# Two norm sums, eight spills and the row maxima of a two-block transformer kernel moved or recast

## The chip, the cores and the metric

The kernel runs on one core of a Trainium2 chip. The metric is the device time of one execution in microseconds (us). Five engines work side by side and meet at semaphores: TensorE (PE, matrix multiplies into PSUM), VectorE (DVE), ScalarE (ACT), GpSimd (POOL) and SyncE (SP, which here issues the weight loads). Each runs its own list of instructions in order.

## What is computed

The reference applies two blocks one after the other to a sequence of 1024 tokens of width 1024, all in float32. The first block mixes banded attention, a convolution and a recurrence, adds a feed-forward part and ends with a norm:

```
def hybrid_layer(x, ...):
    h = rmsnorm(x, norm1_g)
    z = jnp.einsum("bsd,dc->bsc", h, w_in)
    ...
    x = x + jnp.einsum("bsc,cd->bsd", mix, w_out)
    h2 = rmsnorm(x, norm2_g)
    ff = jnp.square(jax.nn.relu(jnp.einsum("bsd,df->bsf", h2, w_up)))
    return x + jnp.einsum("bsf,fd->bsd", ff, w_down)
```

The result goes through `rmsnorm(x, final_g)`. The second block puts 16 learned tokens in front (1040 in all) and runs two layers:

```
for l in range(DEPTH_2):
    h = rmsnorm_2(h_res, norm_gain[l])
    proj = h @ w_in[l]
    u_pool, z_pool, c_q, c_kv, k_rope, z_mla, g_pool, g_mla = jnp.split(proj, ...)
    y_pool = (pool_mix(u_pool, ...) * jax.nn.silu(z_pool)) @ pool_w_up[l]
    o_mla = mla(c_q, c_kv, k_rope, pos, ...)
    ...
    h_res = h_res + merged @ w_out[l]
```

`pool_mix` subtracts each value from running means over 2, 4, 8 and 16 steps, in four groups. `mla` is causal softmax attention with 8 heads; its softmax takes the maximum of each row of scores off before the exponential.

## The kernel before

Activations lie transposed: 128 channels on the partitions, time along the columns, in eight tiles. `X` is the residual, `Ah` and `Al` the rounded high and the low part of the normed activations, `R` 19 work rows (rows 8 to 15 are also `G`, the split inputs of small products), `S_` single columns. A float32 product is made of three rounded (fp32r) matmuls, high by high, high by low and low by high (`chunk_products`, L444; `piece_products`, L549). Weights come as a stream of units of 512 KB through two slots: SP loads one, POOL splits it into high (L388, L400) and low (L379) when the unit before it in the slot is used up. A unit is 128 output channels; its products accumulate in one of two slots of PSUM, `acc[:, 0]` and `acc[:, 1]`, which ACT or DVE must empty before the slot is taken again (`take`).

**Norms at the seams.** Where a residual is finished and normed at once, work goes in column pieces: two for attention's output (`CUTS1`, 512 columns each) and three around the second block (`CUTS_MID`, `CUTS2`, 348 each). `close_two` or `close_down` finish the residual piece by piece; `norm_pieces` on DVE and ACT adds the squares, and with the scale makes `Ah` and `Al` chunk by chunk (eight chunks of a piece); `open_two` on PE multiplies the chunks as they come by the next two units. The sum over channels is one f32 matmul with ones for each piece, `sum_piece` (L546). `open_two` first takes chunks 0 to 3 of piece 0 for unit 0, then the last piece's `sum_piece(n - 1)`, then for k = 0 to 7 unit 0's chunk k + 4 and unit 1's chunk k, and then the further pieces. The order of DVE and ACT is written out by hand:

```
NORM_ORDER = {
    2: (("add", 0), ("norm", 0, 0, 4), ("add", 1), ("norm", 0, 4, 6), ("norm", 0, 6, 8), ("norm", 1, 0, 8)),
...
NORM_SCALE_AFTER = {2: (0, 3), 3: (0, 3, 6)}
```

After the step with such a number ACT waits for the sum of the next piece and makes its scale (L1178, L1182). Within a "norm" step DVE multiplies (L1742), ACT copies to the high part (L1115) and DVE subtracts for the low part (L1735).

**The first layer's two norms.** The second block's first norm is taken of the first block's output before that output's own norm is applied, so two totals of squares are kept: the weighed one for the layer's norm, and the plain one (`R` row 16) for `final_g`. The plain total gets its last two squares after `norm_pieces` (L1430 on ACT, L2067 on DVE), PE sums it in two halves of 512 (L818, four instructions) after the wide unit j = 2, ACT makes the scale in `residual_scale` (L1443, L1446) after its eviction 1, DVE scales the eight residual tiles in `SPILL_ORDER` (L2071), and ACT spills them to DRAM (L1458) after its eviction 3. The pooling (`pool_mix`, L2086 to L2096 in DVE's list) writes over residual tiles, so it waits for all spills. It is followed by L2101, which empties the PSUM slot of the unit j = 4 and the next; PE wants that slot for j = 6. In the second layer the residual is spilled in one piece after the norm (L1436).

**The heads.** The 8 heads of a layer are interleaved: while head h is weighed, head g = h + 1 is projected and normed. PE, DVE and ACT each walk through 15 block steps n of a head with their own hand-written lists. Rough scores (one rounded product, L935 and L939) give the row maxima by `maximum` on DVE (L2219); `turn_maxima` on PE (L956) turns them from columns into a row, in three turns of a head: pc 0 at n = 10 of the head before, pc 1 at n = 0, pc 2 at n = 5. A turn has three f32 matmuls, each with one column of `S_` as weights and 128 columns of the identity moving (20 for the last tile of pc 2). ACT copies the row from partition 32 into row 32 of the queries. `rough_scores` for tile i also waits for `q_hi`, the cast L2198 in `query_norm`. `query_table` starts with L2185.

Of the kernel before, what the change touches and what calls it, by code (L numbers as in the profile page):

```python
# [10 lines left out]
ALU = mybir.AluOpType  # L11
# [137 lines left out]
def build(nc, xT, metaT, pos, params, consts, bands, lru_w, wstream, outT):  # L149
    with ExitStack() as ctx:  # L150
# [59 lines left out]
        extra0 = idr0 + 3 * P  # L210
# [216 lines left out]
        def _(pe):  # L427
# [176 lines left out]
            def open_two(ws, pieces, cuts):  # L604

                n, w = pieces
                lo0 = c["piece_lo"].n
                free0 = c["piece_free"].n
                c["piece_lo"].step(n * KC)
                c["piece_free"].step(2 * (n - 1))  # L610
                ahead = 4

                def begin(p, s):
                    if p < n - 1:
                        pe.wait_ge(sems["piece_free"], free0 + 2 * p + s + 1)
                    else:
                        take(s)

                def arrived(p, k):
                    pe.wait_ge(sems["piece_lo"], lo0 + KC * p + k + 1)  # L620

                next_unit()
                begin(0, 0)
                for k in range(ahead):
                    arrived(0, k)
                    piece_products(0, ws[0], 0, w, k, k == 0, False, (0, 1))
                await_low()
                for k in range(ahead):
                    piece_products(0, ws[0], 0, w, k, False, False, (2,))
                sum_piece(n - 1, cuts)  # L630
                next_unit()
                begin(0, 1)
                for k in range(KC):
                    if k + ahead < KC:
                        arrived(0, k + ahead)
                        piece_products(0, ws[0], 0, w, k + ahead, False, k + ahead == KC - 1)
                    piece_products(1, ws[1], 0, w, k, k == 0, False, (0, 1))
                await_low()
                for k in range(KC):
                    piece_products(1, ws[1], 0, w, k, False, k == KC - 1, (2,))  # L640
                for p in range(1, n):
                    for k in range(KC):
                        for s in range(2):
                            if k == 0:
                                begin(p, s)
                            if s == 0:
                                arrived(p, k)
                            ins = piece_products(s, ws[s], p, w, k, k == 0, k == KC - 1)
                            if p == n - 1 and k == KC - 1:
                                ins.then_inc(sems["unit_done"], 1)  # L650
# [152 lines left out]
            for l in range(LAYERS):  # L803
# [6 lines left out]
                open_two((ws(), ws()), PIECES2, CUTS_MID if l == 0 else CUTS2)  # L810
                for j in range(2, 8):
                    wide(j % 2, ws(), PIECES2)
                    if l == 0 and j == 2:
                        pe.wait_ge(sems["x1_total"], 1)
                        pe.wait_ge(sems["piece_scale"], c["piece_total"].value())
                        for p in range(2):
                            take_aux(p)
                            ins = nc.tensor.matmul(aux[:, p, :], ones, R[:, 16, CUTS1[p]:CUTS1[p + 1]],  # L818
                                                   start=True, stop=True)
                        ins.then_inc(sems["x1_summed"], 1)  # L820
# [123 lines left out]
                def turn_maxima(h, pc):  # L944
# [8 lines left out]
                    for i in range(3 * pc, 3 * pc + 3):  # L953
                        n = min(P, TP - P * i)
                        o = P * (i - 3 * pc)
                        ins = nc.tensor.matmul(acc_r[bank][32:33, o:o + n], S_[:, 16 + i:17 + i], ident[:, P - n:P],  # L956
# [130 lines left out]
        def _(act):  # L1087
# [337 lines left out]
            for l in range(LAYERS):  # L1425
                last = l == LAYERS - 1
                if l == 0:
                    norm_pieces(CUTS_MID, gain_root)
                    for s in range(2):
                        do(nc.scalar.activation(R[:, 13 + s, mid], X[:, KC - 2 + s, mid], ACT.Square), "x1_squared")  # L1430
# [24 lines left out]
                if l == 0:  # L1455
                    for i, j in enumerate(SPILL_ORDER):
                        act.wait_ge(sems["x1_done"], i + 1)
                        act.dma_start(spill_x[:, TP * j:TP * j + TP], X[:, j, :]).then_inc(sems["spilled"], 16)  # L1458
# [209 lines left out]
        def _(dve):  # L1668
# [386 lines left out]
            for slots in totals:  # L2055
                dve.wait_ge(sems[slots[3]], KC - 2)
                do(vec.tensor_tensor(slots[0], slots[0], slots[1 + (KC - 3) % 2], ALU.add), slots[3] + "_free")

            wide = slice(0, TP)
            for l in range(LAYERS):  # L2060
                last = l == LAYERS - 1
                if l == 0:
                    norm_pieces(CUTS_MID, lambda j: S_[:, 8 + j:9 + j], down=True)
                    do(vec.memset(R[:, 0:4, 0:16], 0.0), "to_act")
                    for s in range(2):
                        dve.wait_ge(sems["x1_squared"], s + 1)
                        do(vec.tensor_tensor(R[:, 16, mid], R[:, 16, mid], R[:, 13 + s, mid], ALU.add),  # L2067
# [146 lines left out]
                def maximum(h, i, p):  # L2214
# [4 lines left out]
                    do(vec.tensor_reduce(S_[:, col:col + 1], acc_r[rough_bank(i, p)][:, 0:n], AX, ALU.max, negate=True), "rough_max")  # L2219

                def maxima_of(pc):

                    if pc == 1:
                        do(vec.tensor_tensor(S_[:, 20:22], S_[:, 20:22], S_[:, 25:27], ALU.min), "max_ready")
                    else:
                        do(vec.tensor_tensor(S_[:, 24:25], S_[:, 24:25], S_[:, 30:31], ALU.min))
                        do(vec.tensor_tensor(S_[:, 22:25], S_[:, 22:25], S_[:, 27:30], ALU.min), "max_ready")
# [16 lines left out]
                do(vec.tensor_copy(ident_r, ident))  # L2244
                do(vec.tensor_copy(causal_r, C_[:, 384:512]))
# [232 lines left out]
```

## Time and profile before

| what | value |
|---|---|
| three timed runs | 3276.66, 3276.34, 3274.18 us; median 3276.34 |
| the profiled execution | 3276.7 us; span of its instructions 3274.9 us, mean granted clock of PE 0.975 |
| busy share of the span | PE 93%, PE weight loads 82%, DVE 43%, POOL 33%, ACT 23% |
| chain that ended last | PE 84%, DVE 11%, ACT 3%, issue 1% |

The span is the time from the first to the last instruction of the profiled execution; its own time beside it is measured in the same way as the three runs. PE is busy nearly throughout, so what counts is PE's own work, and the places where PE stands and waits for another engine.

### The profile page before, as it was taken

To read this page: it belongs to the slowest core of one execution; us is meant where nothing else is said; L and a number is where in the kernel's file an instruction comes from. 1 tells how busy PE (TensorE), PEld (TensorE's weight loads), DVE (VectorE), ACT (ScalarE), POOL (GpSimd) and SP (SyncE) were. 2 spreads that over 40 slices of the span, in tenths; PEclk is the share of its full clock that TensorE was granted. 3 is DMA by queue.
4 is the path that set the end of the run, shared out by engine and by line. 5 is a ranking of instruction groups with operands and counts; after the bars stand their busy time and mean duration, and the time that the engine had idled before them with its cause. 6 is when DMAs were issued, how large, how long until landed. Compare 5 with 4: busy or idle time off the path is not lost.

```text
span 3274.9 us, 41451 instructions
## 1 busy us (share of the span) xinstructions
PE 3041.6 (93%) x16392; PEld 2685.3 (82%) x16392; DVE 1424.4 (43%) x1818; ACT 738.0 (23%) x1332; POOL 1066.9 (33%) x1335
## 2 busy tenths in 40 slices
PE   6986679999999998699999899999999999899999
PEld 4764557777777787699999788889999999788899
DVE  4658456332222227520111666673720021766661
ACT  2143322000000003100110455511200111555510
POOL 2523013544444443333332211133433333211132
PEclk9998789999999999899999999999999999999999
DMA  2101011111111111211212000051211212100052
GB/s 107 45 33 36 1 71 46 52 45 49 47 45 45 45 52 33 98 39 46 99 51 79 33 14 14 14 190 39 105 52 46 98 46 81 37 14 14 14 183 78
DMA packets 47447, 182.62 MB, mean 56 GB/s; under 512 B 6081, under 2 KB 6209, under 8 KB 46913
## 3 DMA queue, kind: packets, MB, share of 16 engines
q1 hardware_dynamic: 31248, 113.19, 10.5%
q10 hardware_dynamic: 16048, 67.28, 5.4%
q8 instruction: 113, 1.85, 0.2%
q14 instruction: 38, 0.30, 0.0%
HBM read 150.06 MB, written 30.39 MB: 55 GB/s over the span
## 4 chain that ended last, share of the span: by engine, by line
PE 84%; DVE 11%; ACT 3%; issue 1%; DMA 0%; ACTq 0%; POOL 0%; DVEq 0%; SPq 0%; POOLq 0%
PE acc L451 60%; PE aux L1002 4%; PE acc L886 4%; PE acc L981 3%; PE acc L554 3%; PE acc L935 2%; PE acc L870 1%; PE acc L956 1%; DVE residual L1812 1%; PE acc L898 1%; DVE act_lo L1703 1%; PE acc L908 1%; PE acc L753 1%; DVE act_hi L1702 1%; DVE work L1742 1%
## 5 line engine op out<-in xcount | busy, mean ns | idle before, releaser
L379 POOL TENSOR_TENSOR w_lo<-w_raw,w_hi 128x256 fp32r<-128x256 f32 (+1 forms) x924 | 807.2, 905 | 17.2
L451 PE MATMUL acc<-act_hi,w_hi 128*128 128x348 f32 (+1 forms) x2896 | 712.5, 346 | 61.4 <-DVE work L2101 24.0
L451 PE MATMUL acc<-act_lo,w_hi 128*128 128x348 f32 (+1 forms) x2896 | 708.6, 345 | 0.0
L451 PEld LDWEIGHTS acc<-act_hi,w_hi 128*128 128x128 f32 x2896 | 507.1, 189 | 111.0 <-issue 55.0
L451 PE MATMUL acc<-act_hi,w_lo 128*128 128x348 f32 (+1 forms) x2896 | 562.3, 344 | 0.0
L399 POOL TENSOR_TENSOR small<-shape_consts 128x1 f32<-128x1 f32 x192 | 45.8, 239 | 1530.2 <-PE acc L451 1420.4
L451 PEld LDWEIGHTS acc<-act_lo,w_hi 128*128 128x128 f32 x2896 | 508.7, 189 | 39.8
L451 PEld LDWEIGHTS acc<-act_hi,w_lo 128*128 128x128 f32 x2896 | 490.3, 188 | 39.5
L451 PE MATMUL acc<-ff_split,w_hi 128*128 128x512 f32 (+1 forms) x1376 | 309.9, 374 | 10.8 <-DVE ff_split L1703 10.8
L451 PEld LDWEIGHTS acc<-ff_split,w_hi 128*128 128x128 f32 x1376 | 246.9, 188 | 58.0 <-DVE ff_split L1703 15.0
L1962 DVE TENSOR_TENSOR residual<-acc,residual 128x1024 f32<-128x1024 f32 (+1 forms) x82 | 100.7, 1228 | 389.8 <-PE acc L451 389.8
L388 POOL CAST w_hi<-w_raw 128x1024 fp32r<-128x1024 f32 x23 | 24.8, 1080 | 637.1 <-PE acc L886 548.5
L2219 DVE TENSOR_REDUCE small<-acc 128x1 f32<-128x512 f32 (+4 forms) x240 | 132.2, 551 | 193.6 <-PE acc L939 121.2
L981 PE MATMUL acc<-ff_split 128*128 128x276 f32 (+5 forms) x864 | 208.4, 354 | 0.0
L400 POOL CAST w_hi<-w_raw 128x1024 fp32r<-128x1024 f32 x192 | 201.4, 1049 | 0.0
L1002 PE MATMUL aux<-work 128*128 128x276 f32 (+5 forms) x576 | 177.2, 404 | 0.0
L981 PEld LDWEIGHTS acc<-ff_split 128*128 128x128 f32 x864 | 140.8, 190 | 31.4 <-ACT work L1593 0.5
L1369 ACT ACTIVATE work<-acc 128x1024 f32<-128x1024 f32 x32 | 32.8, 1028 | 580.2 <-PE acc L451 574.6
L451 PE MATMUL acc<-ff_split,w_lo 128*128 128x512 f32 (+1 forms) x688 | 162.7, 373 | 0.0
L1593 ACT ACTIVATE work<-acc 128x384 f32<-128x384 f32 (+2 forms) x240 | 104.4, 436 | 233.2 <-PE acc L981 161.5
L2011 DVE TENSOR_TENSOR work<-work 128x1024 f32<-128x1024 f32 x32 | 40.7, 1273 | 239.2 <-ACT work L1369 239.1
L1115 ACT ACTIVATE work<-acc 64x384 f32<-64x384 f32 (+5 forms) x153 | 93.4, 620 | 225.3 <-PE acc L451 184.7
(277 smaller groups left out, 3791.1 us busy)
## 6 DMA issues: line engine op xcount, KB each, us to landing
w_raw<-in_wstream SPq DMA_DIRECT2D x215, 512.0 KB, 3.3
spill_m<-residual ACTq DMA_DIRECT2D x2, 4176.0 KB, 13.9
spill_g<-work ACTq DMA_DIRECT2D x16, 522.0 KB, 2.7
residual<-spill_m ACTq DMA_DIRECT2D x16, 522.0 KB, 5.6
work<-spill_g ACTq DMA_DIRECT2D x16, 522.0 KB, 7.9
residual<-spill_x ACTq DMA_DIRECT2D x16, 522.0 KB, 4.2
spill_x<-residual ACTq DMA_DIRECT2D x8, 522.0 KB, 5.2
spill_x<-residual ACTq DMA_DIRECT2D x1, 4176.0 KB, 13.2
```

Source lines behind the costliest of these rows:

```text
L379: ins = nc.gpsimd.tensor_tensor(Wl[:, s, c0:c0 + w], Wraw[:, s, c0:c0 + w], Wh[:, s, c0:c0 + w].bitcast(F32), ALU.subtract)
L400: nc.gpsimd.tensor_copy(Wh[:, s, :], Wraw[:, s, :]).then_inc(sems["w_hi_done"], 1)
L451: ins = nc.tensor.matmul(acc[0:m, s, p, 0:w], wt[:, ws, w0 + j * m:w0 + j * m + m], x[:, k, p * w:p * w + w], start=(first and t == 0), st ...
L554: ins = nc.tensor.matmul(acc[:, s, p, 0:w], wt[:, ws, k * P:k * P + P], x[:, k, p * w:p * w + w], start=(first and t == 0), stop=(end and ...
L886: ins = nc.tensor.matmul(acc_q[:, 0:w], wt[:, w_head[0], j * P:j * P + P], x[:, j, c0:c0 + w], start=(j == 0 and t == 0), stop=(j == 5 and ...
L935: ins = nc.tensor.matmul(acc_r[bank][:, 0:n], qh[:, min(P * i, LASTQ):min(P * i, LASTQ) + P], kh[:, 512 * p:512 * p + n], start=True, stop ...
L981: ins = nc.tensor.matmul(out, k2[kt][:, c0:c0 + P], q2[qt][:, lo:lo + w], start=m == 0, stop=(m == 2 and not diag))
L1002: ins = nc.tensor.matmul(aux[:, b % 2, lo - QP * pc:lo - QP * pc + w], values(h)[:, t, :], prob(k)[:, at:at + w], start=t == 0, stop=end)
L1115: return nc.scalar.activation(out, in_, ACT.Copy, scale=scale)
L1593: do(nc.scalar.activation(prob(k)[:, 0:w], src, ACT.Exp), "p_in")
L1962: do(vec.tensor_tensor(x, acc_view(s, pieces), x, ALU.add), f"free{s}")
L2219: do(vec.tensor_reduce(S_[:, col:col + 1], acc_r[rough_bank(i, p)][:, 0:n], AX, ALU.max, negate=True), "rough_max")
```

## The change

It moves three things and recasts one.

- The plain total's sum (L818 before) is taken directly after the opening pair of units, no longer after the unit j = 2. For that one of the two final additions (L2057), the plain total's, moves from before `norm_pieces` to behind it (`last_of`), and the last two squares go to work rows 15 and 13 instead of 13 and 14.
- ACT issues the eight spills directly after `residual_scale`, within the eviction j = 1, so ahead of the evictions 2 and 3.
- In `open_two`, `sum_piece(n - 1)` moves behind the products of k = 1 in the opening with two pieces and of k = 7 in those with three.
- The row maxima are kept in an fp32r area `row_max` of 9 groups of 34 columns, of which column 32 holds the maximum and the rest is zero; a turn's matmul takes the 34 columns as weights and the rounded identity, in one rounded pass, and writes partitions 0 to 33. The area is cleared once a layer, and the scratch `rope_tmp` lies 306 columns further on.

```diff
@@ open_two (PE)
-                sum_piece(n - 1, cuts)
                 next_unit()
                 begin(0, 1)
                 for k in range(KC):
                     if k + ahead < KC:
                         arrived(0, k + ahead)
                         piece_products(0, ws[0], 0, w, k + ahead, False, k + ahead == KC - 1)
                     piece_products(1, ws[1], 0, w, k, k == 0, False, (0, 1))
+                    if k == (1 if n == 2 else KC - 1):
+                        sum_piece(n - 1, cuts)
@@ layers (PE)
                 open_two((ws(), ws()), PIECES2, CUTS_MID if l == 0 else CUTS2)
+                if l == 0:
+                    pe.wait_ge(sems["x1_total"], 1)
+                    pe.wait_ge(sems["piece_scale"], c["piece_total"].value())
+                    for p in range(2):
+                        take_aux(p)
+                        ins = nc.tensor.matmul(aux[:, p, :], ones, R[:, 16, CUTS1[p]:CUTS1[p + 1]],
+                                               start=True, stop=True)
+                    ins.then_inc(sems["x1_summed"], 1)
                 for j in range(2, 8):
                     wide(j % 2, ws(), PIECES2)
-                    if l == 0 and j == 2:
...
@@ turn_maxima (PE)
-                        ins = nc.tensor.matmul(acc_r[bank][32:33, o:o + n], S_[:, 16 + i:17 + i], ident[:, P - n:P],
+                        ins = nc.tensor.matmul(acc_r[bank][0:34, o:o + n], row_max[:, 34 * i:34 * i + 34], ident_r[:, P - n:P],
@@ evictions (ACT)
                     if l == 0 and j == 1:
                         residual_scale()
-                if l == 0:
-                    for i, j in enumerate(SPILL_ORDER):
-                        act.wait_ge(sems["x1_done"], i + 1)
-                        act.dma_start(spill_x[:, TP * j:TP * j + TP], X[:, j, :]).then_inc(sems["spilled"], 16)
+                        for i, t in enumerate(SPILL_ORDER):
+                            act.wait_ge(sems["x1_done"], i + 1)
+                            act.dma_start(spill_x[:, TP * t:TP * t + TP], X[:, t, :]).then_inc(sems["spilled"], 16)
@@ before the layers (DVE)
-            for slots in totals:
+            def last_of(slots):
+
                 dve.wait_ge(sems[slots[3]], KC - 2)
                 do(vec.tensor_tensor(slots[0], slots[0], slots[1 + (KC - 3) % 2], ALU.add), slots[3] + "_free")
+
+            last_of(totals[0])
@@ layers (DVE)
                     norm_pieces(CUTS_MID, lambda j: S_[:, 8 + j:9 + j], down=True)
                     do(vec.memset(R[:, 0:4, 0:16], 0.0), "to_act")
+                    last_of(totals[1])
                     for s in range(2):
                         dve.wait_ge(sems["x1_squared"], s + 1)
-                        do(vec.tensor_tensor(R[:, 16, mid], R[:, 16, mid], R[:, 13 + s, mid], ALU.add),
+                        do(vec.tensor_tensor(R[:, 16, mid], R[:, 16, mid], R[:, 15 - 2 * s, mid], ALU.add),
@@ maximum, maxima_of, head setup (DVE)
+                    to = row_max[:, 34 * i + 32:34 * i + 33] if i < 4 else S_[:, col:col + 1]
...
+                        do(vec.tensor_tensor(row_max[:, 34 * 4 + 32:34 * 5 + 33:34], S_[:, 20:22], S_[:, 25:27], ALU.min), "max_ready")
...
+                do(vec.tensor_scalar(row_max, C_[:, 0:34 * TB], 0.0, None, ALU.mult))
```

## Rows read from the trace of the kernel before

**Rows 1.** Timeline of PE, both layers: start us, us, engine, line, operation, [idle before].

```profile
1274.06 1.47 PE L546 MATMUL aux<-work,shape_consts 128*128 128x332 f32 x2 [3.49 <-DVE work L1728]
...
1292.93 1.51 PE L546 MATMUL aux<-work,shape_consts 128*128 128x344 f32 x2 [6.67 <-DVE work L1728]
...
1389.06 1.21 PE L451 MATMUL acc<-act_hi,w_hi 128*128 128x348 f32 x3 [24.01 <-DVE work L2101]
...
2298.58 0.85 PE L546 MATMUL aux<-work,shape_consts 128*128 128x348 f32 x2 [2.65 <-DVE work L1728]
...
2368.75 0.64 PE L451 MATMUL acc<-act_hi,w_hi 128*128 128x348 f32 x3
```

**Rows 2.** The chain of waits, 1255 to 1400 us: start us, us, what.

```profile
1270.07 1.66 DVE work L2057
...
1317.27 11.72 PE acc L451 x72
1328.99 1.73 PE aux L818 x4
```

**Rows 3.** Timeline of DVE, first layer.

```profile
1310.59 1.11 DVE L1735 TENSOR_TENSOR act_lo<-work,act_hi 128x344 fp32r<-128x344 f32 x2
...
1312.14 2.49 DVE L2067 TENSOR_TENSOR work<-work 128x1024 f32<-128x1024 f32 x2 [0.24 <-ACT work L1430]
1333.21 11.32 DVE L2071 SCALAR_TENSOR_TENSOR residual<-residual,params,work 128x1024 f32<-128x1024 f32 x8 [18.59 <-ACT work L1446]
1356.55 1.70 DVE L2086 TENSOR_TENSOR residual<-work 128x1059 f32<-128x1059 f32 x1 [12.02 <-DMA spill_x<-residual]
...
1387.67 2.52 DVE L2101 TENSOR_TENSOR work<-acc,work 128x1044 f32<-128x1044 f32 x2
```

**Rows 4.** Timeline of DVE, second layer.

```profile
2330.25 1.26 DVE L2086 TENSOR_TENSOR residual<-work 128x1059 f32<-128x1059 f32 x1 [11.94 <-DMA spill_x<-residual]
...
2365.97 1.25 DVE L2101 TENSOR_TENSOR work<-acc,work 128x1044 f32<-128x1044 f32 x1
```

**Rows 5.** The eight spills' line, L1458, by itself.

```profile
DMA to landing us min/median/max: 2.7/5.2/7.5
```

**Rows 6.** Timeline of PE, attention's opening.

```profile
550.04 1.12 PE L546 MATMUL aux<-work,shape_consts 128*128 128x512 f32 x2 [2.01 <-DVE work L1728]
552.43 0.76 PE L554 MATMUL acc<-act_hi,w_hi 128*128 128x512 f32 x1 [1.27 <-DVE act_lo L1735]
...
556.34 0.40 PE L554 MATMUL acc<-act_hi,w_hi 128*128 128x512 f32 x1
```

**Rows 7.** Timeline of ACT, attention's opening.

```profile
552.13 0.67 ACT L1178 ACTIVATE work<-aux,small 128x512 f32<-128x512 f32 x1
...
553.84 0.63 ACT L1115 ACTIVATE act_hi<-work 128x512 fp32r<-128x512 f32 x1 [0.38 <-DVE work L1742]
```

**Rows 8.** Timeline of PE, a turn and its successors; rounded 128-column matmuls elsewhere.

```profile
1834.62 0.82 PE L956 MATMUL acc<-shape_consts,small 128*1 128x128 f32 x6
...
1835.60 0.29 PE L886 MATMUL acc<-act_lo,w_hi 128*128 128x276 f32 x1
...
1926.71 0.50 PE L981 MATMUL acc<-ff_split 128*128 128x128 f32 x3
1927.05 0.27 PE L985 MATMUL acc<-pool_split 128*128 128x128 f32 x1
```

**Rows 9.** Timeline of PE, rough scores after turn 2 and after turn 0.

```profile
1984.83 0.23 PE L935 MATMUL acc<-ff_split 128*128 128x128 f32 x1
...
1997.70 0.47 PE L935 MATMUL acc<-ff_split 128*128 128x512 f32 x1 [0.35 <-issue]
```

**Rows 10.** Timeline of DVE, start of the heads and two query casts.

```profile
1823.04 0.56 DVE L2185 TENSOR_TENSOR residual<-acc,work 128x384 f32<-128x384 f32 x1 [4.14 <-ACT residual L1540]
...
1984.15 0.36 DVE L2198 CAST ff_split<-residual 128x384 fp32r<-128x384 f32 x1
...
1997.24 0.36 DVE L2198 CAST ff_split<-residual 128x384 fp32r<-128x384 f32 x1
```

More of the change, by code:

```diff
@@ L209, in build @@
         ident_r, causal_r, after_r = (G_[:, idr0 + P * i:idr0 + P * i + P] for i in range(3))
-        extra0 = idr0 + 3 * P
+        row_max = G_[:, idr0 + 3 * P:idr0 + 3 * P + 34 * TB]
+        extra0 = idr0 + 3 * P + 34 * TB
         assert extra0 + QP <= 8 * RW
@@ L810, in _ @@
                 open_two((ws(), ws()), PIECES2, CUTS_MID if l == 0 else CUTS2)
+                if l == 0:
[6 more added lines that the diff above has]
+                    ins.then_inc(sems["x1_summed"], 1)
                 for j in range(2, 8):
                     wide(j % 2, ws(), PIECES2)
-                    if l == 0 and j == 2:
[L814 to L820, printed above, removed]
                 next_unit()
@@ L1429, in _ @@
                     for s in range(2):
-                        do(nc.scalar.activation(R[:, 13 + s, mid], X[:, KC - 2 + s, mid], ACT.Square), "x1_squared")
+                        do(nc.scalar.activation(R[:, 15 - 2 * s, mid], X[:, KC - 2 + s, mid], ACT.Square), "x1_squared")
                 else:
@@ L2218, in maximum @@
                     dve.wait_ge(sems["rough_ready"], rough_no(l, h, i, p))
-                    do(vec.tensor_reduce(S_[:, col:col + 1], acc_r[rough_bank(i, p)][:, 0:n], AX, ALU.max, negate=True), "rough_max")
+                    to = row_max[:, 34 * i + 32:34 * i + 33] if i < 4 else S_[:, col:col + 1]
+                    do(vec.tensor_reduce(to, acc_r[rough_bank(i, p)][:, 0:n], AX, ALU.max, negate=True), "rough_max")
                 def maxima_of(pc):
                     if pc == 1:
-                        do(vec.tensor_tensor(S_[:, 20:22], S_[:, 20:22], S_[:, 25:27], ALU.min), "max_ready")
+                        do(vec.tensor_tensor(row_max[:, 34 * 4 + 32:34 * 5 + 33:34], S_[:, 20:22], S_[:, 25:27], ALU.min), "max_ready")
                     else:
                         do(vec.tensor_tensor(S_[:, 24:25], S_[:, 24:25], S_[:, 30:31], ALU.min))
-                        do(vec.tensor_tensor(S_[:, 22:25], S_[:, 22:25], S_[:, 27:30], ALU.min), "max_ready")
+                        do(vec.tensor_tensor(row_max[:, 34 * 6 + 32:34 * 8 + 33:34], S_[:, 22:25], S_[:, 27:30], ALU.min), "max_ready")
                 def head_out(h, pc):
```

## The prediction

> **What bounds the kernel now.** I read the table of the page first: TensorE (PE) is busy 93% of the span and carries 84% of the chain that ended last. So a microsecond counts only where PE waits, or where PE itself works less. The waits of PE come next: in the first attention layer one is 24.01 us long, for VectorE's (DVE's) L2101 [rows 1]. The chain of waits through this stretch [rows 2] shows what it is made of, and DVE's timeline [rows 3] gives the spans. DVE finishes the norm's last piece at 1311.7, adds the two squares until 1314.63 and then has nothing to do. PE takes the plain total's sum only at 1328.99, behind `wide(0)` of j = 2. ScalarE (ACT) turns it into a scale, DVE scales the residual's eight tiles from 1333.21 to 1344.5, and the eight spills are issued behind ACT's eviction at 1342.2. The last lands at 1356.5 (12.02 us of idle DVE). Only then do the four pooling blocks run, up to 1387.67, and L2101 frees the accumulator slot that PE has wanted since 1365.05: PE restarts at 1389.06 [rows 1]. The second layer has the same stage without this: the pooling starts at 2330.25 [rows 4] and PE goes on at 2368.75 with nothing to wait for [rows 1].
>
> **Part 1, sum behind the opening and early spills (L818, L1455 to L1458, L2057).** I follow the chain that will end last.
> - One of the two L2057 additions leaves the head of the norm chain: −1.65 us (1.66 in [rows 2]). DVE's next additions then start 1.65 earlier, PE waits 1.8 instead of 3.49 us for L546, and should not fall to its low clock first: L546 took 1.47 at 1274.06, after 3.49 us of waiting, and 0.85 at 2298.58, after 2.65 [rows 1]. I take −0.65. The norm chain ends at 1311.7 − 2.3 = 1309.4.
> - The moved addition comes back behind it (1.23, the size of one L2067 of [rows 3]), then the two L2067 at 1.23. PE will by then have ended the opening (part 2: 1310.4), so GpSimd splits the next weights beside them; additions then take up to 1.66 instead of 1.25 [rows 2, 3]. The total is ready at about 1314.0.
> - PE has waited 3.6 us for it. The four L818 took 1.73 at full clock [rows 2]; at the low one up to 3.4. I take 3.0: 1317.0.
> - ACT's logarithm and exponential: from L818's end at 1330.72 to L2071's start it is 2.5 us [rows 2, 3]. Scale at 1319.5.
> - L2071: eight take 11.3 [rows 3]: until 1330.8. Each lets its spill go at once, instead of waiting for the eviction at 1342.2. A spill takes 2.7 to 7.5 us to land, 5.2 in the median with all eight together [rows 5]; spread 1.4 us apart I take 4.2 for the last: 1335.0, against 1356.5 now.
> - Pooling: 31.1 us in the first layer, mostly with GpSimd idle because PE stood; 35.7 in the second with PE running [rows 3, 4]. The new first layer resembles the second: 1335.0 + 35.7 = 1370.7, plus L2101 at 1.26 and a hand-over: PE restarts at 1372.1 instead of 1389.06, **−17.0 us**. Bounds: 31.1 for the pooling, 2.7 for the landing and L818 at full clock give −24; 7.5 for the landing and 1 us more for the sums give −13. PE's own work allows no more than about −25 (the sums at 1317, then four units at 11.5 to 11.7 us [rows 2] until 1364).
>
> What stands behind ACT's wait for each `x1_done`: the evictions of units j = 2 and 3. Unit 2 ends near 1329.5 and PE wants its slot when unit 3 ends, near 1341. ACT is free at 1331, so 10 us of cover. The copies 0 and 1 stand ahead of the wait. SP's weight loads share the DMA engines with the spills, but come one per unit here. The other square buffer (slot 15 for 13 and 14) costs nothing: same instructions.
>
> **Part 2, place of L546 in the openings.** Three openings, and they differ.
> - First layer: L546 waits 6.67 us at 1292.93 [rows 1]. Now PE does the first piece of both units in that time and falls onto the norm chain's heels: it ends 0.96 behind it, at 1310.4. This is inside part 1's sum and adds nothing, since the pooling decides.
> - Second layer: the 2.65 us wait at 2298.58 [rows 1] is filled the same way. But L2101 ends at 2367.2 [rows 4] (the spill there hangs on the norm, not on PE), and PE now takes the slot at 2368.75: at most 1.5, **−1.3 us**.
> - Attention's opening (n = 2) loses. ACT's list is fixed by `NORM_SCALE_AFTER[2]`: it waits for the second piece's sum after copies 4 and 5 and before copies 6 and 7. Today L546 runs at 550.04 and ACT passes at 552.13, in time [rows 6, 7]. Now L546 stands behind chunk 5, where PE is at 556.34 [rows 6]. Then L546 1.1, logarithm and exponential 1.3, copy 0.6 [rows 7], DVE's subtraction 0.7 (0.55 for 344 columns in [rows 3], scaled): chunk 6 arrives at 560.1 and PE, there at 556.34, loses 3.8. The restart costs clock: a product lasts 0.76 at 552.43 and 0.40 at 556.34 [rows 6]. Together **+4.5 us**; from +1, if only L546's own time is added, to +6. The block behind it is bound by PE, so it stays.
>
> **Part 3, row maxima (48 turns).** One turn is three f32 matmuls in six instructions: from 1834.62 to 1835.60, less one 0.13 of L886, 0.85 us [rows 8]. The new ones are three instructions in one pass, with 34 columns of weights. No row shows that form. Nearest are the rounded 128-column ones with full weights, 0.113 apart: (1927.05 − 1926.71) / 3 [rows 8]; so at most 0.34 a turn. From below: half of a two-pass instruction, 0.74 / 6 / 2 = 0.06, so 0.18. I take 0.27, near the upper row, since the shape is that but for fewer weights: 0.58 saved a turn (0.51 to 0.67). The Trainium skill ("TensorE: Matmul & The Clock Gate", back-to-back issue gap) gives about 81 ns for each load-and-multiply pair of 128 columns; by it a turn would be 0.24 and the saving 0.61. The trace shows 113 for that pair with full weights.
>
> Where does it go? At 1997.70 PE waits 0.35 for the query cast (L2198, 1997.24 + 0.36), which ends a run of DVE that began with a maximum before the turn [rows 9, 10]. So what turn 0 saves only lengthens this wait: 0. After turn 2, L2198 ends at 1984.51 and PE is there at 1984.83: 0.32 can pass [rows 9, 10]. Turn 1 has nothing of the kind behind it: 0.58. Per layer seven heads with both (0.90 each) and the last one, with DVE behind, 0.2: 6.5; twice: **−13 us** (−9 to −16).
>
> The new clearing of `row_max` (306 columns, once a layer) lies in front of DVE's 4.14 us of idle time [rows 10], and is less than the 0.56 of the 384 columns in the same row: nothing. If that cover went it would be at most +1.2.
>
> **Sum.** −17.0 − 1.3 + 4.5 − 13 = −26.8. The profiled execution took 3276.7 (span 3274.9), 0.4 above the median of 3276.34. So 3249.9 by its measure, 3249.5 by the median's.
>
> **Rivals.**
> - A: every turn passes its saving on, because the DVE runs shrink or start earlier. 48 × 0.58 = 28 instead of 13: 3235. Against it: the wait at 1997.70 is there already. 10%.
> - B: no turn passes anything; DVE and ACT hold the heads. 3262. Against it: the 0.32 of slack after turn 2, and no such wait after turn 1. 10%.
> - C: the spills are bound by transfer or by ACT's queue, so that of part 1 only the earlier sums come through: about 11 instead of 17.0, 3256. For it: 12 us from L2071's end to landing today. Against: today they start with all eight ready at once. 12%.
> - D, the other side: the rounded form runs behind its weight load. A lone 128-column multiply shows 0.27 [rows 8]; as long again for the load, thrice, is 1.6, or 0.75 more than now. On turns 1 and 2 of 16 heads, 32 × 0.75 = +24, in place of −13: 3287. It decides from 1.3 us a turn on (13.8 / 32 = 0.43 above 0.85). 4%.
>
> **How the numbers follow.** The sum as it stands 62%, with its own range 3241 to 3258 from the bounds of parts 1 to 3; A 10, B 10, C 12, D 4, unnamed 2. The range 3236 to 3262 takes in B and C and leaves A and D out. A measurement of this kernel tells 0.2% (6.6 us) from no change: faster 95%, same 2%, slower 3%.
>
> **What the profile after would show.** PE's wait for L2101 near 8 us instead of 24.01; L2086 of the first layer starting near 1335; L2071 ending by 1331. In attention's opening a new PE wait of some 2.8 us for L1735 with ACT waiting for L546 before it. L956 with 144 instructions instead of 288, the wait before L935 at turn 0 grown to about 0.9. The prediction is wrong if the spills still land 12 us after L2071, if no wait appears in attention's opening, or if the L935 waits don't grow.

## The result

The changed kernel takes 3249.63 us (median of 4, 3248.22 to 3251.9) against 3276.5 for the one before: ratio 0.9919, 95% interval 0.9906 to 0.9931, so 26.9 us faster. The forecast was 3249.5, in 3236 to 3262. The profiled execution is the slowest of the four, 3251.9 with a span of 3250.1, which is 24.8 below the 3274.9 of before; so the shares below add up to 24.8.

PE's waits in the profile after (what waited, what for: us in total, times, longest):

```profile
PE acc L937 <- issue: 17.7, 29, 1.1
PE acc L555 <- DVE act_lo L1736: 8.8, 5, 4.4
PE acc L452 <- DVE work L2106: 8.5, 3, 6.2
PE acc L937 <- DVE ff_split L2203: 6.8, 5, 1.9
PE aux L818 <- DVE work L2072: 3.7, 1, 3.7
```

Three of these answer to the parts. L2106 is the L2101 of before: its longest wait fell from 24.01 us [rows 1] to 6.2. L555 (L554 before) has a wait of 4.4, which is the opening of attention. L937 (L935 before) waits 17.7 us in 29 places that look like nothing ("issue"), which is the query cast in the heads. PE's timeline shows each of them in its place, first attention's opening, then the first layer:

```profile
552.87 0.77 PE L555 MATMUL acc<-act_hi,w_hi 128*128 128x512 f32 x1 [4.39 <-DVE act_lo L1736]
...
556.79 1.02 PE L547 MATMUL aux<-work,shape_consts 128*128 128x512 f32 x2
560.56 0.50 PE L555 MATMUL acc<-act_hi,w_hi 128*128 128x512 f32 x1 [2.75 <-DVE act_lo L1736]
...
1318.69 3.78 PE L818 MATMUL aux<-work,shape_consts 128*128 128x512 f32 x4 [3.66 <-DVE work L2072]
...
1375.32 1.21 PE L452 MATMUL acc<-act_hi,w_hi 128*128 128x348 f32 x3 [6.20 <-DVE work L2106]
```

and DVE's timeline of the same layer, beside [rows 3]:

```profile
1324.97 10.53 DVE L2076 SCALAR_TENSOR_TENSOR residual<-residual,params,work 128x1024 f32<-128x1024 f32 x8 [6.33 <-ACT work L1448]
1339.00 1.54 DVE L2091 TENSOR_TENSOR residual<-work 128x1059 f32<-128x1059 f32 x1 [3.50 <-DMA spill_x<-residual]
...
1373.93 2.53 DVE L2106 TENSOR_TENSOR work<-acc,work 128x1044 f32<-128x1044 f32 x2
```

The pooling's wait for the spills is 3.50 us where it was 12.02. In the heads, PE and DVE show the turns and the two waits (L958 is the turn, L956 before; L2203 the query cast, L2198 before):

```profile
1968.73 0.30 PE L937 MATMUL acc<-ff_split 128*128 128x128 f32 x1 [0.15 <-issue]
...
1977.75 0.34 PE L958 MATMUL acc<-pool_split 128*34 128x128 f32 x3
1977.93 0.68 PE L1004 MATMUL aux<-work 128*128 128x276 f32 x2
...
1979.85 0.75 PE L983 MATMUL acc<-ff_split 128*128 128x276 f32 x3
1981.67 0.47 PE L937 MATMUL acc<-ff_split 128*128 128x512 f32 x1 [1.07 <-issue]
```

```profile
1968.27 0.36 DVE L2203 CAST ff_split<-residual 128x384 fp32r<-128x384 f32 x1
...
1981.21 0.36 DVE L2203 CAST ff_split<-residual 128x384 fp32r<-128x384 f32 x1
```

A turn is 1977.93 - 1977.75 = 0.18 us from its start to its successor's. The cast ends at 1981.57 and L937 starts 0.10 later: the wait is the cast's.

**Where the 24.8 us went.** Two traces are compared by the distance between the same two instructions in each, since the absolute times also carry what happened earlier. The marks are the first L1742 of attention's opening (537.18 before, 537.62 after), the last L1962 ahead of the first layer (1264.19 and 1268.47), PE's restart behind L2101 (1389.06 and 1375.32), the first and last turn of each layer (1834.62 to 2139.29, and 1821.14 to 2120.72; 2813.06 to 3117.99, and 2794.05 to 3093.64), the first L546 of the second layer (2279.28 and 2259.86), and its last L2101 (2393.03 and 2371.46).

| stretch | forecast | after less before |
|---|---|---|
| start to attention's opening | 0 | +0.4 |
| attention's opening | +4.5 | +3.8 |
| first layer to PE's restart | -17.0 | -18.0 |
| restart to the first turn | 0 | +0.3 |
| heads, both layers, and what follows to the next mark | -13 | -11.7 |
| second layer's opening and pooling | -1.3 | -2.2 |
| from there to the second layer's first turn | 0 | +2.6 |

The last row has no edit in it. The windows view of the entry into the second layer's heads, from PE's first product behind a wait of 5.6 us (L898 before, L900 after) to the first turn, before and after (stretch: us, then busy us of PE, PEld, DVE, ACT and POOL, then PE's granted clock, DMA share, GB/s):

```profile
2797.29:2813.06 15.77, 13.44 (x57) 9.74 (x58) 8.07 (x17) 7.51 (x15) 0.00 (x0) 0.86 0.08 29
```

```profile
2775.70:2794.05 18.35, 16.55 (x56) 12.77 (x57) 8.20 (x18) 7.50 (x15) 0.00 (x0) 0.65 0.06 24
```

The same work, after the same wait, takes PE 15.77 us at a mean granted clock of 0.86 before and 18.35 us at 0.65 after (means over 2.4 GHz and the lower 1.2 GHz). These are the 2.6 us: they are PE's clock, in a stretch that no edit touches. The 14 profiled executions of this case have 28 such entries, two in each. 20 of them take 15.5 to 15.8 us at 0.86 to 0.91, and 8 take 17.7 to 18.4 us at 0.65 to 0.68, in kernels with and without each edit. What decides between the two is not shown: a kernel shifts the entry in time, and whether all executions of one kernel go the same way was not seen.

### The profile page after: what moved, and what is told of

Its sections match the earlier page's. It is cut to its first block, busy times and chain, and to the rows that moved or that the text cites. A ratio compares the mean times of both kernels' runs of the same rounds, so it can differ in the third digit from the quotient of the medians.

```text
span 3250.1 us, 41165 instructions
## 1 busy us (share of the span) xinstructions
PE 3021.2 (93%) x16248; PEld 2676.3 (82%) x16248; DVE 1429.1 (44%) x1820; ACT 736.8 (23%) x1332; POOL 1070.1 (33%) x1335
## 3 DMA queue, kind: packets, MB, share of 16 engines
q1 hardware_dynamic: 31248, 113.19, 10.5%
## 4 chain that ended last, share of the span: by engine, by line
PE 83%; DVE 12%; ACT 3%; issue 2%; DMA 0%; POOL 0%; DVEq 0%; ACTq 0%; SPq 0%; POOLq 0%
PE acc L452 60%; PE acc L888 4%; PE aux L1004 4%; PE acc L983 3%; PE acc L555 2%; PE acc L937 2%; PE acc L872 1%; DVE residual L1813 1%; PE acc L900 1%; DVE act_lo L1704 1%; DVE act_lo L1736 1%; DVE work L1743 1%; PE acc L910 1%; PE acc L755 1%; DVE act_hi L1703 1%
## 5 line engine op out<-in xcount | busy, mean ns | idle before, releaser
L452 PE MATMUL acc<-act_hi,w_hi 128*128 128x348 f32 (+1 forms) x2896 | 713.6, 347 | 43.3 <-ACT residual L1211 13.2
L389 POOL CAST w_hi<-w_raw 128x1024 fp32r<-128x1024 f32 x23 | 24.8, 1078 | 628.6 <-PE acc L888 541.6
L983 PE MATMUL acc<-ff_split 128*128 128x276 f32 (+5 forms) x864 | 208.4, 354 | 0.1
L983 PEld LDWEIGHTS acc<-ff_split 128*128 128x128 f32 x864 | 140.6, 190 | 31.6 <-issue 0.7
L2225 DVE TENSOR_REDUCE small<-acc 128x1 f32<-128x512 f32 (+4 forms) x176 | 100.7, 572 | 101.4 <-PE acc L937 57.5
## 6 DMA issues: line engine op xcount, KB each, us to landing
spill_m<-residual ACTq DMA_DIRECT2D x2, 4176.0 KB, 13.2
spill_x<-residual ACTq DMA_DIRECT2D x1, 4176.0 KB, 12.3
```

The source lines that it names most:

```text
L452: ins = nc.tensor.matmul(acc[0:m, s, p, 0:w], wt[:, ws, w0 + j * m:w0 + j * m + m], x[:, k, p * w:p * w + w], start=(first and t == 0), st ...
L983: ins = nc.tensor.matmul(out, k2[kt][:, c0:c0 + P], q2[qt][:, lo:lo + w], start=m == 0, stop=(m == 2 and not diag))
L2225: do(vec.tensor_reduce(to, acc_r[rough_bank(i, p)][:, 0:n], AX, ALU.max, negate=True), "rough_max")
```

## The experiments

In all of them "before" and "after" are the two kernels of this case. Twelve kernels ran; the times are medians, with 3276.1, 3276.9 and 3276.7 us for the kernel before in the three groups, so times of different groups are comparable to some 0.8 us.

**1. The sum of attention's opening back in its old place** (from after; a_sum2_back)

```diff
+                if n == 2:
+                    sum_piece(n - 1, cuts)
                 next_unit()
                 begin(0, 1)
...
-                    if k == (1 if n == 2 else KC - 1):
+                    if n != 2 and k == KC - 1:
```

> The changed kernel with the last piece's sum of attention's opening (the one with two pieces) back ahead of the second unit; the two openings with three pieces keep the new place. Theory: the changed kernel lost 4.3 us here (its 2.75 us stop of PE behind the moved sum, and work at the low clock), so this one takes 3249.6 - 4.3 = 3245.3 us, the 2.75 us stop is gone and PE waits some 2.0 us before the sum and 1.3 behind it, as before the change. Rival: the loss is given back later because VectorE's norm of the second piece sets the end of the opening either way; then 3249.6.

Measured: 3246.64 (ratio to before 0.991, 0.9894 to 0.9927), 3.0 below after. PE's timeline of this kernel:

```profile
549.97 1.13 PE L547 MATMUL aux<-work,shape_consts 128*128 128x512 f32 x2 [1.99 <-DVE work L1731]
552.36 0.76 PE L555 MATMUL acc<-act_hi,w_hi 128*128 128x512 f32 x1 [1.26 <-DVE act_lo L1738]
```

The second stop is gone and both waits of [rows 6] are back. Between the marks of this stretch it takes 726.98 us (537.11 to 1264.09), before took 727.01 and after 730.85: the whole 3.84 is the new place of this one sum.

**2. The early sums and spills, together and each alone** (from before; b_part1, b_sums, b_spills). b_part1 has the edits to L818, L2057, L2067, L1430 and L1455 to L1458 of the diff, and nothing in `open_two` or the heads; b_sums leaves the spills behind eviction 3; b_spills has only the spills.

> The kernel before with only the sums and the spills changed (the plain total's sum behind the opening, its last addition behind the norm's pieces, spills ahead of evictions 2 and 3). Theory: the changed kernel gained 18.0 us here. Without the new place of the piece's sum PE ends the opening later (1317.3 less some 2.3) and meets a total that is ready, so the four instructions of the sum run at full clock (1.7 us instead of 3.8) and the pooling starts another 1.5 us earlier: 3276.5 - 19.5 = 3257.0. Rival one: nothing hangs on that, -18.0, 3258.5. Rival two: the new place of the piece's sum is what let the sum come early, and without it the gain is 15 or less.

> The kernel before with the early sums only; the spills stay behind ScalarE's eviction 3. Theory: the residual is scaled by about 1330, but the spills still wait for eviction 3, which ends when PE ends unit 3, only 2.3 us earlier than before: the gain is 2.3 us, 3274.2. Rival: the spills move with the scaled tiles and this part alone carries most of the 18 us.

> The kernel before with the early issue of the spills only; the sum stays behind unit 2. Theory: the residual is scaled until 1344.5 as before, each spill goes at once and the last lands at about 1348, 8 us earlier; ScalarE comes to the evictions 2 and 3 only then, so PE stops some 3.6 us after unit 3, and the pooling runs beside more of PE's work. In all 3.5 to 8 us, 5.7 taken: 3270.8. With the sums alone (2.3) that is 8, not 18: the two parts need each other. Rival: the parts simply add, then this one must give 16 us.

**3. With the place of the three-piece sum, and that place alone** (b_part1_n3 is b_part1 with it, b_n3 is before with it)

```diff
-                sum_piece(n - 1, cuts)
+                if n == 2:
+                    sum_piece(n - 1, cuts)
...
                     piece_products(1, ws[1], 0, w, k, k == 0, False, (0, 1))
+                    if n != 2 and k == KC - 1:
+                        sum_piece(n - 1, cuts)
```

> The early sums and spills on the kernel before (3263.3 us by themselves) together with the new place of the piece's sum in the two openings with three pieces; attention's opening and the row maxima stay as before. Theory: the place of that sum is worth some 4 us in the first layer, because PE ends the opening earlier, GpSimd splits the next two units' weights beside the sums and is done when VectorE scales the residual: the eight L2071 of the line take 10.5 us as in the changed kernel, not 13.6, and the pooling starts 3.4 us earlier. With 0.6 in the second layer: 3263.3 - 4.3 = 3259.0. Rival: as in my prediction, the place adds nothing in the first layer; then 3262.7 or the loss of the sums alone has another cause, and the scaling takes 13.6 us still.

> The kernel before with nothing but the new place of the piece's sum in the two openings with three pieces. Theory: PE ends the first layer's opening some 3.3 us earlier, so unit 2, and the plain total's sum behind it, come 3.3 us earlier, and with them the scaling, the spills, the pooling and PE's restart; 0.6 us more in the second layer: 3276.3 - 3.9 = 3272.4. Rival, as in my prediction: nothing in the first layer and 1.3 in the second, 3275.0. If the place pays only by taking GpSimd's splits away from the scaling, which does not collide with them in the kernel before, the first layer gives less than 1 us.

PE's restart in b_part1, b_sums, b_spills, b_part1_n3 and b_n3, one timeline each:

```profile
1375.20 1.21 PE L451 MATMUL acc<-act_hi,w_hi 128*128 128x348 f32 x3 [11.82 <-DVE work L2104]
```

```profile
1386.55 1.21 PE L451 MATMUL acc<-act_hi,w_hi 128*128 128x348 f32 x3 [23.99 <-DVE work L2105]
```

```profile
1381.01 1.21 PE L451 MATMUL acc<-act_hi,w_hi 128*128 128x348 f32 x3 [11.50 <-DVE work L2100]
```

```profile
1368.39 1.21 PE L451 MATMUL acc<-act_hi,w_hi 128*128 128x348 f32 x3 [6.09 <-DVE work L2107]
```

```profile
1385.15 1.21 PE L451 MATMUL acc<-act_hi,w_hi 128*128 128x348 f32 x3 [23.98 <-DVE work L2104]
```

Less the start of the last add ahead of the layer (1264.72, 1263.88, 1262.20, 1261.57 and 1263.10), and less the 124.87 of before, these are the gains in the first layer:

| kernel | in the first layer | median, and less before's |
|---|---|---|
| sums alone | -2.2 | 3276.67, +0.6 |
| spills alone | -6.1 | 3273.05, -3.0 |
| sums and spills | -14.4 | 3263.3, -12.8 |
| three-piece place alone | -2.8 | 3277.58, +0.8 |
| all three | -18.1 | 3257.94, -18.9 |
| after | -18.0 | |

Not all of a gain in the first layer reaches the end of the kernel. In the profiled execution of b_spills the entry into the first heads took 17.78 us, where before took 15.60; in that of b_sums the second layer's opening and pooling took 114.89 us, where before took 113.75.

Neither half of part 1 is worth much alone: -2.2 and -6.1 make -8.3, together they give -14.4. Without the early issue the spills start behind the eviction at 1339.70 (ACT's timeline of b_sums) although the residual is scaled by 1333; without the early sum there is nothing to spill before 1331, and the evictions queued behind the spills stop PE for 3.96 us (PE's timeline of b_spills, second fence):

```profile
1339.69 1.04 ACT L1115 ACTIVATE work<-acc 128x1044 f32<-128x1044 f32 x1 [10.41 <-PE acc L451]
1339.70 8.57 ACTq L1458 DMA_DIRECT2D spill_x<-residual  x8
```

```profile
1344.14 1.21 PE L451 MATMUL acc<-act_hi,w_hi 128*128 128x348 f32 x3 [3.96 <-ACT work L1115]
```

The expectation for b_part1 was wrong by 5 us in this layer (19.5 expected, 14.4 measured) and by 6.3 in the median, and so was its reason. PE did meet a ready total and summed it in 1.88 us instead of 3.78, so the scale came earlier. But then the scaling of the residual was slow. The windows view of that line's eight instructions in b_part1, in b_part1_n3 and in after (columns as above, POOL's busy time standing before the granted clock):

```profile
1320.08:1333.64 13.56, 13.56 (x88) 13.56 (x86) 13.31 (x8) 0.00 (x0) 11.68 (x9) 1.00 0.84 311
```

```profile
1318.05:1328.58 10.53, 10.53 (x69) 10.53 (x67) 10.28 (x8) 0.00 (x0) 0.49 (x2) 1.00 0.92 360
```

```profile
1324.97:1335.50 10.53, 10.53 (x68) 10.53 (x67) 10.28 (x8) 0.00 (x0) 0.59 (x2) 1.00 0.90 356
```

POOL is busy 11.68 of 13.56 us beside the scaling in b_part1, 0.49 and 0.59 of 10.53 in the other two, and an L2071 takes 1.65 us in the median there against 1.285. When PE ends the opening earlier, POOL splits the next two units beside the sums and is through: its first split starts 10.3 us ahead of the scaling in after (1314.71 and 1324.97), 4.5 us ahead in b_part1 (1315.54 and 1320.08). So the place of the three-piece sum is worth 3.7 us here (18.1 less 14.4), where the expectation of b_part1_n3 has some 4. Of b_part1's stages, counted from the same mark, the scaling starts 1.1 us earlier than in b_part1_n3 and takes 3.0 longer, the wait for the last spill behind it is 1.2 longer (4.84 against 3.61) and the pooling 0.5. POOL's share is shown for the scaling; why the last spill lands later behind it is not. The Trainium skill ("GPSIMD Engine Reference", Specifications) says that GpSimd shares its SBUF interfaces with VectorE, with contention for VectorE's instructions that read two SBUF inputs. By that rule these instructions, with a residual tile and the scale from SBUF, should suffer, and the trace agrees: 1.65 against 1.285 us.

b_n3 was expected at 3272.4 and came out at 3277.58. Its gain is there in the first layer, 2.8 us, and the kernel is no faster. The windows view of before and of b_n3 at the entry into the first layer's heads, again from the product behind the wait to the first turn:

```profile
1819.02:1834.62 15.60, 13.08 (x57) 9.60 (x57) 8.06 (x17) 7.40 (x15) 0.00 (x0) 0.90 0.07 28
```

```profile
1816.37:1834.19 17.82, 16.01 (x57) 12.09 (x57) 8.06 (x17) 7.52 (x15) 0.00 (x0) 0.68 0.07 25
```

That is 2.2 us more for the same work, at 0.68 of the clock where it was 0.90, and at the second entry it is 2.5 us more (18.23 against 15.77, at 0.66). In the profiled execution these 4.7 us use up the gain. Whether each timed run of b_n3 loses it in the same way was not seen, only that ten of them have a median at before's.

**4. Which turns count** (from after; a_turn0_x4 and a_turn1_x4: the three instructions of one turn issued four times)

```diff
-                    for i in range(3 * pc, 3 * pc + 3):
+                    for i in list(range(3 * pc, 3 * pc + 3)) * (4 if pc == 0 else 1):
```

> The changed kernel with the three instructions of turn 0 issued four times over (the same values written again): 9 more of 0.057 us, 0.51 us a head. Theory: what turn 0 costs or saves ends in PE's wait for the query's cast (1.07 us at 1981.67), so the wait shrinks to 0.56 and the time stays: 3249.6 plus at most 1. Rival: every turn passes its time on, 16 x 0.51 = 8.2, 3257.8.

> The same for turn 1. Theory: nothing behind it absorbs anything but what the turn 2 wait takes (0.15 us), which it reaches as well: of 0.51 us a head 0.36 to 0.51 come through, 16 x 0.36 to 0.51 = 5.8 to 8.2, so 3255.4 to 3257.8. Rival: VectorE holds the heads in any case, 0 to 2.

Measured: 3251.35 and 3257.19, 1.7 and 7.6 above after. The period of a head, from a turn 0 to the next, says it without the noise of the rest. Turns 1 and 2 of the same head lie between. PE's timeline of before, of after, of a_turn0_x4 and of a_turn1_x4:

```profile
1953.10 0.81 PE L956 MATMUL acc<-shape_consts,small 128*1 128x128 f32 x6
...
1965.80 0.82 PE L956 MATMUL acc<-shape_consts,small 128*1 128x128 f32 x6
...
1980.53 0.64 PE L956 MATMUL acc<-shape_consts,small 128*1 128x128 f32 x6
...
1993.88 0.82 PE L956 MATMUL acc<-shape_consts,small 128*1 128x128 f32 x6
```

```profile
1937.79 0.34 PE L958 MATMUL acc<-pool_split 128*34 128x128 f32 x3
...
1950.52 0.34 PE L958 MATMUL acc<-pool_split 128*34 128x128 f32 x3
...
1964.56 0.29 PE L958 MATMUL acc<-pool_split 128*34 128x128 f32 x3
```

```profile
1938.85 0.89 PE L958 MATMUL acc<-pool_split 128*34 128x128 f32 x12
...
1978.81 0.88 PE L958 MATMUL acc<-pool_split 128*34 128x128 f32 x12
...
1982.73 0.47 PE L937 MATMUL acc<-ff_split 128*128 128x512 f32 x1 [0.55 <-issue]
```

```profile
1936.60 0.34 PE L958 MATMUL acc<-pool_split 128*34 128x128 f32 x3
...
1977.10 0.34 PE L958 MATMUL acc<-pool_split 128*34 128x128 f32 x3
1989.84 0.88 PE L958 MATMUL acc<-pool_split 128*34 128x128 f32 x12
```

Before 40.78, after 39.96 (to 1977.75), turn 0 fourfold 39.96, turn 1 fourfold 40.50. Nine more instructions at turn 0 cost nothing and take 0.52 us off the wait of 1.07; at turn 1 they cost 0.54 us a head. The 1.7 us of a_turn0_x4 are therefore not the turns'. Its profiled execution is not longer than that of after (span 3249.5 against 3250.1) and differs outside the heads: the first entry took 17.66 us (15.66 in after) and the second 15.67 (18.35), and in the second layer the one spill took 13.6 us to land (12.3), so that PE waited 0.76 us for L2106. What separates the medians the runs don't say.

The distances from turn 0 to 1, 1 to 2 and 2 to 0 are 12.70, 14.73 and 13.35 us before and 12.73, 14.04 and 13.19 after: turn 0 gives nothing, turn 1 0.69 and turn 2 0.16.

**5. Wider weights in a turn** (from after; a_turn64: 64 columns instead of 34; a single execution, 3251.78)

> The changed kernel with 64 columns of weights instead of 34 in each maximum's instruction (row_max[:, 34 * i:34 * i + 64]; the last tile keeps 34). A turn of three takes 0.18 us now, 0.057 apart; the rounded 128-column products with 128 columns of weights lie 0.113 apart. Theory: the weights' columns set the pace, so 64 of them lie 0.057 x 64 / 34 = 0.11 apart or somewhere between the two, and turn 1 takes at least 0.05 us more a turn. Rival: the columns of the moving side set it (128 at 2.4 GHz are 0.053), the weights are hidden behind, and nothing moves, 0.18 a turn.

```profile
1990.35 0.35 PE L959 MATMUL acc<-pool_split 128*64 128x128 f32 x3
1990.53 0.68 PE L1005 MATMUL aux<-work 128*128 128x276 f32 x2
```

```profile
L959 PEld LDWEIGHTS acc<-pool_split 128*64 128x64 f32 x62 | 7.0, 134 | 0.5
```

The load takes 134 ns instead of the 109 of 34 columns, and the turn 0.18 us as with 34 (1990.53 less 1990.35): the rival was right. The Trainium skill ("TensorE: Matmul & The Clock Gate", Back-to-back issue gap) also gives, for a single product apart from the sustained rate, columns divided by 2.4 plus 2.5 ns, which for 128 is 56; the trace's 0.18 / 3 = 60 ns stands nearer to that than to its 81 for a sustained pair.

**6. The query's cast ahead of `head_out`** (from after; a_order)

```diff
                             if n in (6, 11):
                                 query_norm(g, n // 5 - 1)
+                                if h >= 0:
+                                    head_out(h, n // 5 - 1)
...
-                            if n == 10:
+                            if n == 10 and not more:
                                 head_out(h, 1)
```

(and the same condition on `head_out(h, 0)` at n = 6).

> The changed kernel with two steps of VectorE's list exchanged in the heads: query_norm(g, 0) before head_out(h, 0), and query_norm(g, 1) before head_out(h, 1), so that the query's cast comes 1.15 us earlier. Theory: PE's waits of 1.07 us after turn 0 and 0.15 us after turn 2 are waits for that cast alone, and its scale from ScalarE is ready (1977.40, VectorE comes to it at 1979.4): 14 heads x 1.22 = 17 us at most; the maxima behind head_out come no earlier, so part may return as waits for a rough-score bank: 8 to 17, 14 taken, 3235.6. Rival: another wait (ScalarE's query scale, or a bank) ends at the same time, and less than 4 us come.

Measured: 3226.4 (ratio 0.9844, 0.9828 to 0.9861), 23.2 below after. PE's timeline of this kernel:

```profile
1974.37 0.74 PE L983 MATMUL acc<-ff_split 128*128 128x276 f32 x3
1975.01 0.47 PE L937 MATMUL acc<-ff_split 128*128 128x512 f32 x1
```

Both waits are gone, but the gain is larger than the 17 us of both waits, which the expectation had as the most that could come (14 taken). From the last L983 to L937 it is 0.64 us here and was 1.82 (1979.85 to 1981.67), so the wait shown as 1.07 cost 1.18; the wait shown as 0.15 cost 0.38 in the same way (from L983 to the L941 that follows L937: 1.12 against 0.74). The two make 1.56 us a head, 22 us in 14 heads, and the period of a head is 38.41 where it was 39.96. The rest of the 23.2 is within what the clock at the entries moves.

**7. Both gains, and one more wait removed** (a_best is a_order with experiment 1; a_best_inv also takes `inverse_sums(h, 1)` on ACT from n = 9 to n = 10)

> The two gains together: the exchanged order of query_norm and head_out on VectorE, and the sum of attention's opening at its old place. They lie in stages far apart and must add: 3226.4 - 3.0 to 4.0 = 3222.4 to 3223.4.

> The same with inverse_sums(h, 1) on ScalarE behind the query's scale and the block's exponents (n = 10 instead of 9). PE's L872 waits 0.38 us in each head for the scale's first activation (L1562), which stands behind the two of inverse_sums; it would come 0.65 us earlier. A wait that goes gave about 0.2 us more than its length in the last runs, so 14 x (0.38 + 0.2) = 8 us: 3214.5. Rival: VectorE's head_out gets its factor later and PE waits for it, or the exponents come later: 3 us or less.

Measured: 3221.67 and 3222.49. The first beats both kernels of the case: ratio to before 0.9834 (0.9818 to 0.9851), 28.0 below after, 4.7 below a_order where 3 to 4 was expected. The second gained nothing. PE's timeline of a_best, and of a_best_inv, one head:

```profile
1965.40 0.39 PE L874 MATMUL acc<-act_hi,w_hi 128*128 128x276 f32 x1 [0.39 <-ACT residual L1564]
...
1969.01 0.47 PE L939 MATMUL acc<-ff_split 128*128 128x512 f32 x1
```

```profile
1970.23 0.39 PE L874 MATMUL acc<-act_hi,w_hi 128*128 128x276 f32 x1
...
1974.38 0.48 PE L939 MATMUL acc<-ff_split 128*128 128x512 f32 x1 [0.45 <-issue]
```

The wait of 0.39 us is gone and one of 0.45 stands 4 us later, again the query's cast: PE came earlier to a DVE that had not moved. The period of a head is the same to 0.02 us.

## Why the prediction was right

The time came out 0.1 us from the forecast, partly by luck: four terms were each off by 0.7 to 1.3 us, with both signs, and the clock moved single runs by more. By the profiled execution, where the terms can be added up, it is 3251.9 against the 3249.9 forecast. The range of the sum, 3241 to 3258, is narrower than its own bounds: -24 to -13, -1.3, +1 to +6 and -16 to -9 add up to 3236 to 3259.

- **Part 1, first layer.** Forecast -17.0, measured -18.0, and the chain held step by step. Taken back by the 4.28 us by which this layer started later, the sum started at 1314.4 (forecast 1314.0), ended at 1318.2 (1317.0; its four instructions took 3.78 at the low clock and not 3.0), the scaling ended at 1331.2 (1330.8), the pooling started at 1334.7 (1335.0), and PE restarted at 1371.0 (1372.1). The low clock of the sum is shown: PE was granted 0.50 in these 3.78 us. The pooling took 34.9 us from its first L2091 to L2106, near the 35.7 of the second layer, as taken, and not the 31.1 of the first. Rival C is out: the spills landed 3.5 us after the last scaling, not 12.
- **Part 2, three pieces.** "Adds nothing" in the first layer was right only because the -17.0 had PE's early end of the opening in it (1310.4). Taken by itself the place is worth 3.7 us there, most of it by way of POOL's splits, which no longer lie beside the scaling: the prediction kept 11.3 us for the scaling, and it took 10.5. In the second layer 1.5 of the 2.2 us are clock: b_part1, which leaves that opening alone, has the same stretch 1.54 us shorter than before (2265.88 to 2378.09 against 2279.28 to 2393.03), at a granted clock of 1.00 instead of 0.94. The edit makes PE end the opening 0.6 us earlier (its first product behind the opening comes 41.4 us after the mark, 42.0 in b_part1), but with it alone only 0.15 to 0.17 us reach the end of the stretch (112.04 us in b_n3 and 112.06 in b_part1_n3, against 112.21 in b_part1, all at 1.00), because PE then waits 0.2 us for the first L2101. In after it does not wait: the spill landed in 12.3 us instead of 13.1 or 13.2, the pooling started 0.8 us sooner and the stretch took 111.60. Why that spill landed sooner is open. So the term was 0.2 by itself and at most 0.6, not 1.3; the 1.5 us by which PE came behind L2101 in before [rows 1, 4] were there at that trace's lower clock.
- **Part 2, two pieces.** +4.5 was forecast, +3.84 measured. The new stop was forecast as some 2.8 us and is 2.75, and ends at 560.56, or 560.12 less the 0.44 by which this stage starts later, where chunk 6 was expected at 560.1. The restart cost less: the first product behind it took 0.50 us and the next ones 0.39, at a granted clock of 1.00.
- **Part 3.** Forecast -13, measured -11.7, and the three turns behave as said: nothing from turn 0 (the wait of 0.35 grew to 1.07, forecast 0.9), part of turn 2, all of turn 1. Two sizes were off. A turn takes 0.18 us, the lower bound, not the 0.27 I took because the nearest row's shape had 128 columns of weights; so turn 1 gives 0.69 and not 0.58. And turn 2 gives 0.16 and not 0.32. It is 0.43 us shorter (from 0.57, 1980.53 to 1981.10, to 0.14, 1964.56 to 1964.70), but then PE runs into the cast, and from L983 to the L941 behind it it takes 1.12 us where before took 0.73 (1984.16 to 1984.89): slack of 0.32 is not all gain once PE has to stop at its end. Rivals A, B and D are out.
- **Not in the sum**: the clock at the entry of the second layer's heads, +2.6 us in the profiled execution, and the +0.4 and +0.3 us of two stretches without an edit.

## What to carry to other kernels

Before pricing a shorter instruction, find the next thing that its engine waits for: the saving stops there, and repeating the instruction fourfold shows whether anything is left, if it is read from the distance between two marks in the same stage and not from the time of the kernel. Where a saving disappears into a wait, the step to change is the one that the wait is for; here exchanging two steps of another engine's list was worth nearly as much as the whole change (23.2 us against 26.9). And two edits on one chain can be worth little each and much together, so an edit that measures nothing alone isn't done with.

## What the hardware showed beyond that

- Two short waits of PE cost more than the profile shows: 1.18 us for one shown as 1.07, 0.38 for one shown as 0.15.
- Three rounded products of 128 columns take 0.18 us whether 34 or 64 columns of weights are loaded (109 and 134 ns a load), while with 128 columns of weights they lie 0.113 apart [rows 8].
- After the same wait of 5.6 us the same stretch of products ran at a granted clock of 0.86 to 0.91 or of 0.65 to 0.68, in kernels that do not differ there, and took 15.5 to 15.8 or 17.7 to 18.4 us. The distance between two marks inside one stage (40.78, 39.96, 40.50 and 38.4 us a head) tells far smaller differences than the time of the whole kernel.
- The eight 128 x 1024 scalings of VectorE took 1.285 us each beside a GpSimd that was busy 0.59 of 10.53 us, and 1.65 us in the median beside one busy 11.68 of 13.56.
